# A mixed decoder step with a mixture of experts on one core: the loop nest that counts an expert's blocks, three levels with computed bounds against two with fixed ones

## The reference, cut to what matters

```python
logits = h @ w_router + b_router
top_v, top_i = top_k(logits, 4)
gates = softmax(top_v)
for every token and each of its 4 experts e:
    a = h @ w1[e] + b1[e]                     # 1024 -> 2048
    x_glu = min(a[:, :1024], 7.0)
    x_lin = clip(a[:, 1024:], -7.0, 7.0)
    mid = x_glu * sigmoid(1.702 * x_glu) * (x_lin + 1.0)
    out[token] += gate * (mid @ w2[e] + b2[e])
```

## Time and profile before

| | |
|---|---|
| median of 3 runs | 1308.63 us (1305.98 to 1311.66) |
| the profiled execution | 1308.63 us, its span 1306.8 us |
| TensorE matmuls | busy 1146.5 us (88%) |
| TensorE weight loads | busy 442.0 us (34%) |
| VectorE | busy 576.2 us (44%) |
| ScalarE | busy 223.2 us (17%) |
| GpSimd | busy 80.4 us (6%) |
| DMA queue of SP | 444.87 MB, 84.5% of 16 engines' span |
| chain that ended last | PE 55%, DVE 11%, DMA 10%, SPq 8%, issue 6%, DVEq 4% |

### The profile page before, as it was taken

The page is one execution under the profiler, slowest core; times in us unless marked ns, Lnnn a source line. Parts: engine busy times, 40 slices in busy tenths (PEclk is TensorE's granted clock), DMA queues, the critical chain, the costliest instruction groups (busy, mean ns, idle before and its releaser), DMA issues.

```text
span 1306.8 us, 25968 instructions
## 1 busy us (share of the span) xinstructions
PE 1146.5 (88%) x8837; PEld 442.0 (34%) x8838; DVE 576.2 (44%) x1306; ACT 223.2 (17%) x428; POOL 80.4 (6%) x188
## 2 busy tenths in 40 slices
PE   5999788979998899989998996899999977999984
PEld 4765444433332233323232331233233322333321
DVE  4999844443342433444243433233343332433443
ACT  3102433131110111111111111111111110111112
POOL 2268300000000000000000000000000000000000
PEclk9999998959999999999999999899999989999998
DMA  9425592870799998998999999979997999799994
GB/s 245 151 78 175 192 340 95 346 282 0 292 420 421 421 376 363 421 422 336 391 422 421 421 422 421 422 325 421 422 421 297 421 421 422 325 420 423 421 418 179
DMA packets 80707, 445.31 MB, mean 341 GB/s; under 512 B 16640, under 2 KB 17728, under 8 KB 31904
## 3 DMA queue, kind: packets, MB, share of 16 engines
q1 hardware_dynamic: 80672, 444.87, 84.5%
HBM read 442.33 MB, written 2.51 MB: 340 GB/s over the span
## 4 chain that ended last, share of the span: by engine, by line
PE 55%; DVE 11%; DMA 10%; SPq 8%; issue 6%; DVEq 4%; ACT 1%; POOL 0%; ACTq 0%
PE ps L1540 21%; PE ps L1529 9%; SPq L464 8%; DMA ring<-in_w_moe_dram 6%; PE ps L1548 6%; PE ps L1555 5%; DMA w_glu<-in_w_moe_dram 4%; PE ps L1567 3%; PE ps L1445 2%; PE ps L1580 1%; PE ps L1564 1%; DVEq L323 1%; DVEq L315 1%; DVE ring L882 1%; DVE ring L887 1%
## 5 line engine op out<-in xcount | busy, mean ns | idle before, releaser
L1540 PE MATMUL ps<-ring,uni 128*32 128x512 f32 x2032 | 230.8, 594 | 6.7 <-DMA ring<-in_w_moe_dram 6.7
L1114 DVE TENSOR_TENSOR x<-x,ps 128x1024 f32<-128x1024 f32 x158 | 186.7, 1210 | 5.4 <-PE ps L1529 4.4
L1135 DVE TENSOR_SCALAR uni<-ps 128x256 f32<-128x256 f32 x51 | 21.7, 425 | 350.0 <-PE ps L1540 350.0
L1529 PE MATMUL ps<-uni 64*128 64x512 f32 x624 | 166.8, 640 | 2.2 <-DVE x L1114 1.3
L1555 PE MATMUL ps<-uni 128*32 128x256 f32 x1224 | 82.3, 405 | 47.5 <-issue 33.9
L1548 PE MATMUL ps<-ring,uni 128*32 128x512 f32 x896 | 104.8, 596 | 20.9 <-DVE uni L1144 15.2
L1540 PEld LDWEIGHTS ps<-ring,uni 128*32 128x32 f32 x2032 | 62.2, 110 | 168.3 <-issue 153.8
L744 ACT ACTIVATE uni<-uni 128x256 f32<-128x256 f32 x51 | 21.3, 417 | 496.8 <-DVE uni L1135 496.8
L1529 PEld LDWEIGHTS ps<-uni 64*128 64x128 f32 x624 | 53.3, 192 | 96.7 <-issue 86.3
L744 ACT ACT_TABLE_LOAD x51 | 65.4, 1283 | 73.3 <-issue 73.2
L1555 PEld LDWEIGHTS ps<-uni 128*32 128x32 f32 x1224 | 38.6, 114 | 109.9 <-issue 65.9
(11 more groups left out here) (363 smaller groups left out, 1220.6 us busy)
## 6 DMA issues: line engine op xcount, KB each, us to landing
ring<-in_w_moe_dram SPq DMA_DIRECT2D x232, 1024.0 KB, 22.6
tmp<-in_w_moe_dram SPq DMA_DIRECT2D x38, 1024.0 KB, 24.4
kv_rows<-in_w_moe_dram SPq DMA_DIRECT2D x19, 1024.0 KB, 22.6
w_glu<-in_w_moe_dram SPq DMA_DIRECT2D x19, 1024.0 KB, 25.3
mixer<-in_w_moe_dram SPq DMA_DIRECT2D x19, 1024.0 KB, 19.1
uni<-in_w_moe_dram SPq DMA_DIRECT2D x19, 1024.0 KB, 21.5
accT<-in_w_moe_dram SPq DMA_DIRECT2D x19, 1024.0 KB, 23.2
low<-in_w_moe_dram SPq DMA_DIRECT2D x19, 1024.0 KB, 24.9
```

Source lines behind the costliest of these rows:

```text
L1114: tt(rows(t), rows(t), ps[0:TILES[t][1], b0:b0 + 2, :], ALU.add).then_inc(S["acc"], 1)
L1529: ins = mm(ps[:, b0 + c, :], selT[rows, P * t:P * t + P], y[rows, :], start=True, stop=True)
L1540: ins = mm(hidden(q), xe[:, k % 2, quarter(k // 2)], slot(turn, k)[:, :, NQ * q:NQ * q + NQ], start=False, stop=(k == 7), skip_group_check ...
```

## The change

The three-level nest gives way to a nest of two levels with fixed bounds. The outer loop `o` is 0, 1, 2 and its test is count > 96 o; the inner loop `c` is 0, 1, 2 with the test count > 96 o + 32 c. The block's first token is 96 o + 32 c. The three lines fewer move all later lines up by three.

```diff
-                with eng.Fori(0, 2 * CAP, CAP) as p:
-                    with eng.If(count > p):
-                        with eng.Fori(p, 2 * p + CAP, CAP) as o:
-                            with eng.If(count > 2 * o - p):
-                                with eng.Fori(2 * o - p, 6 * o - 4 * p + CAP, CAP) as c:
-                                    with eng.If(count > c):
-                                        n = eng.snap(done, min_val=0, max_val=NEXP * CHUNKS)
-                                        first = nc.s_assert_within(c, 0, CHUNKS * CAP - CAP, skip_runtime_bounds_check_because="p, o, c of the three loops give 0; 1, 2; 3 to 8 times CAP")
-                                        block_of(n, turn, name, before, first)
-                                        eng.reg_add(done, done, 1)
+                with eng.Fori(0, 3) as o:
+                    with eng.If(count > o * (3 * CAP)):
+                        with eng.Fori(0, 3) as c:
+                            with eng.If(count > o * (3 * CAP) + c * CAP):
+                                n = eng.snap(done, min_val=0, max_val=NEXP * CHUNKS)
+                                block_of(n, turn, name, before, o * (3 * CAP) + c * CAP)
+                                eng.reg_add(done, done, 1)
```

## The result

| | before | after |
|---|---|---|
| median of 5 runs | 1308.63 us (1305.98 to 1311.66) | 1319.09 us (1317.38 to 1320.57) |
| the profiled execution | 1308.63 us, span 1306.8 | 1320.45 us, span 1318.7 |
| ratio after to before | | 1.0078, 95% interval 1.0055 to 1.0100 |

Slower by 0.8%, some 10 us. The forecast was 1323, its range 1314 to 1331.

A forecast was written before the change was run, and what follows sets the result against it. The prediction took TensorE's pace in three sections between weight-bound stretches to bound the kernel. Gaps +14.1, level points -3.6 and end terms gave +10.2, the clock +5: +15 on 1308.63, said as 1323 us, range 1314 to 1331.

The forecast's parts named there:

- The sections: 470.34 to 621.59, 845.21 to 997.03, 1101.29 to the end: only there does TensorE's pace count, with 7, 4, 3 experts.
- The price behind a one-block expert: TensorE's gap before the next L1555: three more failed rounds less savings, +1.87 us each, bounds 1.5 and 2.2.
- Behind two and three blocks: TensorE's gap behind such experts: one failed round added, 0.63 saved, +0.14 us each.
- Level points: Three places where TensorE has just waited for weights, level with the DMA: shorter walk to a second block, -1.2 us each.
- VectorE: Its selection L1119 before L1555 comes some 1.6 us later per one-block expert, stays behind TensorE's sequencer and adds nothing.
- The end and the entry: Wait for last weights goes, -0.5 us; start of L1529, +0.4; first L1119 sooner on the way in, -0.2.
- The sum without the clock: Gaps in the sections +14.1 us, level points -3.6, end and entry terms: together +10.2.
- The clock: L1555 behind gaps over 2 us meets the 1.2 GHz level one time in two: +5 us, bounds -1.5 and +12.
- The weights cover it: Rival: the weight stream hides the longer gaps, no measurable change, +1 to +6 us, 1308 to 1314; chance 0.07.
- Faster: Rival: failed rounds are cheap and the saved walk, head and closing count, 1300 us with rounds at 0.1; chance 0.02.
- The instruction fetches: Rival: six more taken branches per one-block expert all miss the fetched code, +46 us and more, 1355; chance 0.01.
- The 0.85: Added us per one-block expert if a compare-and-branch takes the skill page's 108 ns; the sum would be an estimated +3.

The follow-up runs named there:

- turns 2 and 4: New nest on all three engines, only for the third and fifth expert of each group of five, against the kernel before: 1312.29 us, ratio 1.0011.
- turns 1 and 3: New nest on all three engines, only for the second and fourth expert of each group of five, against the kernel before: 1323.71 us, ratio 1.0112.
- one round more: Changed kernel with an outer loop of four rounds instead of three: 1344.68 us, ratio 1.0256 to the kernel before.
- one less: Changed kernel with an outer loop of two rounds instead of three: 1308.25 us, ratio 1.0003 to the kernel before.

## Why the prediction was right, and what was mis-sized

**What bounds.** Shown. The sections decide and the rest is covered: the two placements (turns 2 and 4, turns 1 and 3) gave +1.5 and +14.6 us, and over 8 us of longer gaps between the sections left the rest unchanged.

**The price behind a one-block expert.** 1.87 was said; the gaps give 2.64 - 0.91 = 1.73, within the bounds of 1.5 and 2.2. Over 7 experts that is 12.1 instead of 13.1. The round of the outer loop, 0.77, came out as 0.78 (one round more) and 0.81 (one less). The two walks of the earlier trace rows and of the profile after, followed from one sequencer instruction to the next, show where the 0.14 lies. Of the changed kernel's four failed rounds the two inner ones take 0.84 and 0.92 us and the two outer ones 0.75 each, so three rounds more, with their products, are 2.49 where I had 2.51. The closings and the way in save 0.82 where I had 0.63, and the load of the count takes 0.09 more. So the rounds were priced rightly and the fixed saving too small.

**Behind two and three blocks.** +0.14 was said; the seven gaps in the sections grew by 0.01 to 0.08 behind two blocks and by 0.03 to 0.11 behind three. Small.

**Level points.** -1.2 each: 1.07 has become nothing where even the overlap of -0.18 is usual, so -1.25. Right, and it holds only if TensorE itself has the new nest (1.06 is left with VectorE and ScalarE alone).

**VectorE.** "It stays behind the sequencer and adds nothing" holds in the changed kernel. But its reserve was smaller than the rows suggested: alone it opens gaps of up to 1.9. Had TensorE's price been 0.9 lower, VectorE would have been the bound behind four of the seven.

**The end and the entry.** The 0.50 wait is gone, as said; the last adding back starts 0.3 later against what is before it (+0.4 was said); from the last expert's start to the end 36.98 has become 36.57, -0.4 for a forecast of -0.1. On the way in, the gap in front of the first block is 1.28 where 1.51 stood, for a forecast of -0.2.

**The sum without the clock.** From level to end +11.6 was forecast (10.2, and the 1.2 and 0.2 that lie ahead of the level point); 10.5, 10.4 and 10.2 were measured, against the first profile of before; against its second, with the fall in its last adding back taken off, they are 0.7 less. The terms above add up to some 9.7 of the 10.5; 0.7 lies behind the restart at 1002.33, on the way to the third level point. This is the part that the rows gave.

**The clock.** This is the term that was mis-sized: +5, "at one in two". In the profiles it was +7.8, +2.4 and +0.8 (falls less the 1.6 of the first profile of before), so inside its bounds of -1.5 and +12 each time. But the ratios of all runs, +10.2 and +7.2 us, leave it near zero, +1 and -2, beside 10.4 - 1.4 = 9.0 for the rest. Two things made it too large. I took the chance from five starts, three of which had met the lower clock. In all twelve profiles, counted as a gather that took more than 1.54 us, 19 of 55 starts met it behind gaps of 2.5 to 2.75; of the nine gaps over 2 in the sections, five met it in the changed kernel's first profile, two in its second and one with the change on TensorE alone. And I set it against one fall of the kernel before, which in its second profile had two, and a third in the last adding back. Part of the difference between profile and median is also the execution: the changed kernel's first profile has the most falls of the three. Two readings were incomplete: a level start can be slow without any gap (expert 25, 0.7 to 2.1 us of the falls in these three profiles), and "no gap below 2" passed over the stage's first block, whose gather takes 2.79 behind 1.51. The upper bound of +24, too, would be 1333, not the 1331 at which the range ends. The errors of the two terms have the same sign, so no luck of cancelling put the time into the range.

**The rivals.** "The weights cover it" needed 1308 to 1314 and cheap rounds; neither was so. "Faster" needed rounds under 0.4. The instruction fetches are 19 in every profile. The Trainium skill (Runtime: NRT & Kernel Launch, Instruction fetch mechanics) has a taken branch stall when its target lies outside the fetched window; no run here shows such a stall. The Trainium skill (Advanced Engine Details and Errata, Control Flow Timing) has one figure, about 108 ns, for a compare-and-branch. It does not fit the rows of L325 and L326: 76 and 77 ns at least, and 215 and 222 at the median once most are taken. The 0.85 that the prediction works out from it leaves out the 0.06 us between two instructions; with them it is an estimated 1.1, still far from 1.73.

**What stays open.** Why a gap of 2.64 meets the lower clock in one execution and not in the next; no difference in the work before it was found in the traces. And whether the two-level nest would pay where experts have more tokens: no run here had an expert above 96.

## What to carry to other kernels

A loop whose test fails still goes through its failed rounds, here 0.75 to 0.92 us each on TensorE's sequencer, and every engine that has the loop pays its own price; count rounds for the commonest trip count, not for the largest. Price the walk against what the sequencer runs ahead, and only in stretches where that engine sets the pace. These stretches are not fixed: a longer gap uses up the waits between them, and the clock falls more often behind it, so a linear price does not hold for long (the three rounds more of the change, less what it saves, cost 10 us; one more cost 26 on top, two more 60). A run time loop bound takes the failed rounds away altogether.

## What the runs showed of the hardware that was not expected

- Whether the clock falls behind a gap differs from one execution to the next over a wide range of gaps. A gather of more than 1.54 us (1.50 at the full clock) stood behind 0 of 81 gaps of 1.3 to 2.05 us, 14 of 28 of 2.05 to 2.5, 19 of 55 of 2.5 to 2.75, 1 of 2 of 2.75 to 2.9, 14 of 22 of 2.9 to 3.3, 17 of 23 of 3.3 to 3.6, and 29 of 30 from 3.8 on, in twelve profiles. (The expectation of the kernel with one round more counts only gathers above 1.9. The first block of the stage is left out: 2.79 in all twelve, behind 0.78 to 1.52.) A fall mostly costs 1.3 to 1.7 us. The length of the gap is not all: behind gaps under 1.3 or none, 12 of 359 gathers met the lower clock, and in the last adding back, behind 1.32 us of idle time in all twelve, 7 did.
- A branch that is taken costs TensorE's sequencer about three times one that is not: medians of 215 and 222 ns where two of three are taken (L325, L326), 79 where 51 of 96 are not (L328), and least values of 65 to 77.
- Identical code took 288.1 to 294.6 us to its first expert block, over twelve profiles. One profile's span says nothing of a 10 us change until this is taken off.
